# Squares of x moved from ScalarE and VectorE to GpSimd, a PSUM wait moved ahead of the pooling output, and two splits of the last stage issued earlier

## The reference

```python
def rms_norm(x, g):
    xf = x.astype(jnp.float32)
    y = xf * lax.rsqrt(jnp.mean(xf * xf, axis=-1, keepdims=True) + EPS)
    return (y * g.astype(jnp.float32)).astype(x.dtype)
...
    # first layer, with xn = rms_norm(h, pre_norm[0]) and h = x
    z = xn @ w_in
    u, g = jnp.split(z, 2, axis=-1)
    ...                     # pooled: window means of u, minus u, in four groups
    mixed = jnp.einsum('bsgc,gcd->bsgd', pooled, w_group).reshape(B, S, E_POOL)
    return (mixed * scale * jax.nn.silu(g)) @ w_out
...
    # last layer
    return (jax.nn.silu(g) * val) @ w_down
```

## Time and profile before

| | before |
|---|---|
| median of 3 runs | 2605.69 us |
| the profiled execution | 2608.29 us, with a span of 2606.3 us |
| PE busy | 2531.4 us (97%) |
| DVE busy | 1542.0 us (59%) |
| ACT busy | 1324.1 us (51%) |
| POOL busy | 99.4 us (4%) |
| DMA | 450.91 MB, mean 173 GB/s |
| granted TensorE clock, mean | 0.995 |

### The profile page before, as it was taken

The page is one execution under the profiler, slowest core; times in us unless marked ns, Lnnn a source line. Parts: engine busy times, 40 slices in busy tenths (PEclk is TensorE's granted clock), DMA queues, the critical chain, the costliest instruction groups (busy, mean ns, idle before and its releaser), DMA issues. The chain is left out here.

```text
span 2606.3 us, 35319 instructions
## 1 busy us (share of the span) xinstructions
PE 2531.4 (97%) x12930; PEld 2150.1 (82%) x12930; DVE 1542.0 (59%) x1817; ACT 1324.1 (51%) x1752; POOL 99.4 (4%) x156
## 2 busy tenths in 40 slices
PE   8999999999999999999899998899999999999998
PEld 7888888887779887778688887877888888888886
DVE  6665766644655555565555445655666666776554
ACT  5544444544556556464555445445554454554443
POOL 0000000000000001110000002000000000000010
PEclk9999999999999999999999999899999999999999
DMA  8666665555556660565566662054456666656563
GB/s 293 192 188 186 186 187 188 201 193 174 179 157 180 194 192 17 185 235 184 152 184 181 190 191 67 19 170 154 122 170 193 181 190 184 187 172 203 193 201 110
DMA packets 233421, 450.91 MB, mean 173 GB/s; under 512 B 14468, under 2 KB 59728, under 8 KB 232285
## 3 DMA queue, kind: packets, MB, share of 16 engines
q1 hardware_dynamic: 230518, 435.97, 53.9%
q0 software_dynamic: 2624, 13.27, 1.5%
q10 hardware_dynamic: 168, 0.19, 0.0%
HBM read 447.25 MB, written 2.12 MB: 172 GB/s over the span
## 5 line engine op out<-in xcount | busy, mean ns | idle before, releaser
L1445 DVE TENSOR_TENSOR w_lo<-raw,w_hi 128x1024 fp32r<-128x1024 f32 x852 | 1047.2, 1235 | 828.6 <-ACT w_hi L1007 809.7
L1007 ACT ACTIVATE w_hi<-raw 128x1024 fp32r<-128x1024 f32 x852 | 898.7, 1059 | 974.5 <-PE ps L620 616.0
L640 PE MATMUL ps<-x_hi_lo,w_hi 128*128 128x512 f32 x2336 | 823.7, 395 | 13.2 <-DVE w_lo L1445 13.2
L642 PE MATMUL ps<-x_hi_lo,w_lo 128*128 128x256 f32 x2336 | 661.7, 283 | 0.0
L640 PEld LDWEIGHTS ps<-x_hi_lo,w_hi 128*128 128x128 f32 x2336 | 440.0, 188 | 115.8 <-issue 9.0
L618 PE MATMUL ps<-w_hi,x_hi_lo 128*128 128x512 f32 (+3 forms) x1280 | 497.8, 389 | 21.3 <-DVE x_hi_lo L1474 12.4
L620 PE MATMUL ps<-w_hi,x_hi_lo 128*128 128x512 f32 (+3 forms) x1280 | 492.2, 385 | 0.0
L619 PE MATMUL ps<-w_lo,x_hi_lo 128*128 128x512 f32 (+3 forms) x1280 | 490.8, 383 | 0.0
L642 PEld LDWEIGHTS ps<-x_hi_lo,w_lo 128*128 128x128 f32 x2336 | 440.4, 189 | 0.0
L618 PEld LDWEIGHTS ps<-w_hi,x_hi_lo 128*128 128x128 f32 x1280 | 241.0, 188 | 76.7 <-issue 23.9
L620 PEld LDWEIGHTS ps<-w_hi,x_hi_lo 128*128 128x128 f32 x1280 | 240.8, 188 | 42.9
(11 more groups left out here) (306 smaller groups left out, 2237.8 us busy)
## 6 DMA issues: line engine op xcount, KB each, us to landing
raw<-in_w_up SPq DMA_DIRECT2D x160, 512.0 KB, 3.9
raw<-in_pool_w_in SPq DMA_DIRECT2D x128, 512.0 KB, 4.0
raw<-in_w_in SPq DMA_DIRECT2D x96, 480.0 KB, 4.0
raw<-in_w_down SPq DMA_DIRECT2D x76, 512.0 KB, 4.7
raw<-in_pool_w_out SPq DMA_DIRECT2D x64, 512.0 KB, 4.4
raw<-in_ple_w_gate SPq DMA_DIRECT2D x64, 512.0 KB, 3.9
raw<-in_mla_w_in SPq DMA_DIRECT2D x56, 448.0 KB, 4.0
raw<-in_pool_w_group SPq DMA_DIRECT2D x32, 512.0 KB, 4.3
```

Of the source, the lines that this page charges most:

```text
L640: pe.matmul(bank, w_hi[:, slot, cols], xs[:, k].rearrange("p s n -> p (s n)"), start=k == 0, stop=False, skip_group_check=True)
L642: last = pe.matmul(bank[:, 0:T], w_lo[:, slot, cols], xs[:, k, 0, :], start=False, stop=k == nkt - 1, skip_group_check=True)
L1007: act.activation(w_hi[:, u % RING, :], raw[:, slot, :], ACT.Copy).then_inc(S("w_hi"), 1)
L1445: dve.tensor_tensor(w_lo[:, u % RING, :], raw[:, u % RAW, :], w_hi[:, u % RING, :].bitcast(F32), ALU.subtract)\
```

## The change

The change has three parts.

1. *Squares.* ACT loses its eight square instructions and a first tiny copy. DVE loses the two adds. POOL gets seven instructions of 128x1024: a square of four tiles of x into `xsum`, then three times a square into `xsq` and an add onto `xsum`. They wait for the pieces of x and for one another. The loads of h are issued after them. The new tiles lie where `gate_in` and `mixed_group` come later.
2. *PSUM wait.* PE waits for the read-out of both last pooling chunks before the pooling output, no longer before the transposing of h.
3. *Last stage.* `hi(2)` ahead of `y_hi(4)` and `lo(2)` ahead of `y_lo(4)` go; the two units are handled after piece 5.

```diff
+    xsum = arena("x_square_sums", 78592, [128, 4, T])
+    xsq = arena("x_squares", 82688, [128, 4, T])
...
-                    last = pe.matmul(ps[:, 0, 0:T], onesq, xsq[:, n, :], start=n == 0, stop=n == 3)
+                    last = pe.matmul(ps[:, 0, 0:T], onesq, xsum[:, n, :], start=n == 0, stop=n == 3)
...
+        for c in (-2, -1):
+            n = CHUNKS_END["pool"] + c
+            pe.wait_ge(S(f"mm_free{n % 2}"), n // 2 + 2)
         pe.wait_ge(S("ident_in"), 16)
         ready_ple = split_ready("p_split")
         columns(yh, yl, 32, ready=lambda k: pe.wait_ge(S("y_lo"), Y_PIECES.index(k) + 1) if k in Y_PIECES else None)
...
-            if n == 0:
-                last = CHUNKS_END["pool"] - 1
-                pe.wait_ge(S(f"mm_free{last % 2}"), last // 2 + 2)
...
-        act.wait_ge(S("ones_square"), 1)
-        act.activation(junk[:, 0:1], onesq[:, 0:1], ACT.Copy)
         act.wait_ge(S("gains_in"), 16)
...
             split_hi(xh, xt, g, GAIN["pre0"])
             hi(1)
-            last = act.activation(xsq[:, 2 * g:2 * g + 2, :], xt[:, 2 * g:2 * g + 2, :], ACT.Square)
-        last.then_inc(S("x_squared"), 1)
...
-        hi(2)
         y_hi(4)
         hi(1)
         y_hi(5)
         for c in range(NCH):
-            skip(len(units_of(FKT)) - (0 if c else 3))
+            skip(len(units_of(FKT)) - (0 if c else 1))
...
-                lo(1)
-                dve.wait_ge(S("x_squared"), 1)
-                link(dve.tensor_tensor(xsq[:, 0:8, :], xsq[:, 0:8, :], xsq[:, 8:16, :], ALU.add))
-                lo(1)
-                dve.tensor_tensor(xsq[:, 0:4, :], xsq[:, 0:4, :], xsq[:, 4:8, :], ALU.add).then_inc(S("x_summed"), 1)
-                lo(3)
+                lo(5)
...
-        lo(2)
         y_lo(4)
         lo(1)
         y_lo(5)
         for c in range(NCH):
-            add_chunk(chunk(len(units_of(FKT)) - (0 if c else 3)), c * 512)
+            add_chunk(chunk(len(units_of(FKT)) - (0 if c else 1)), c * 512)
...
-        pool.wait_ge(S("x_squared"), 1)
+        for n, k in enumerate((0, 4, 8, 12)):
+            for piece in ((0, 1), (2,), (3,), (4,))[n]:
+                pool.wait_ge(S(f"x_in{piece}"), 16)
+            if n == 0:
+                pool.tensor_tensor(xsum, xt[:, 0:4, :], xt[:, 0:4, :], ALU.mult).then_inc(S("x_squares"), 1)
+            else:
+                pool.tensor_tensor(xsq, xt[:, k:k + 4, :], xt[:, k:k + 4, :], ALU.mult).then_inc(S("x_squares"), 1)
+                pool.wait_ge(S("x_squares"), 2 * n)
+                pool.tensor_tensor(xsum, xsum, xsq, ALU.add).then_inc(S("x_squares"), 1)
+                pool.wait_ge(S("x_squares"), 2 * n + 1)
+        pool.sem_inc(S("x_summed"), 1)
```

More of the change, by code:

```diff
@@ L228, in build @@
     xt = arena("x_features", 88064, [128, KT, T])
-    xsq = arena("x_squares", 32768, [128, KT, T])
+    xsum = arena("x_square_sums", 78592, [128, 4, T])
+    xsq = arena("x_squares", 82688, [128, 4, T])
     phl = arena("pooled_hi_lo", 88064, [128, 8, 2, T], F32R)
```

## The result

The changed kernel is slower: 2624.70 us against 2605.69 us (medians of five runs each), a difference of 19.0 us, with a ratio of 1.0072 (95% interval 1.0056 to 1.0088). One of the five runs of the changed kernel took 5063.95 us, and one of 21 of the kernel before beside the first experiments 5058.16 us, both at a full granted clock and for a reason that no trace here shows; the medians count them, the ratios leave them out. The profiled execution took 2627.47 us against 2608.29, 19.2 more, with a span of 2625.7 us.

What follows compares the result with a forecast made beforehand. PE, busy 97%, was taken as the bound: its stream plus its waits. Terms 0.1 + 11.5 + 1.9 + 2.8 + 2.6 + 1.4 = 20.3 us on the median 2605.69 gave 2626.0 us, range 2612 to 2633.

Steps and rivals of the forecast that it cites:

- Where the loss would be: PE waits at the start for the third and fourth unit, before the pooling output, and three units into the down product.
- (a): Rival, chance 0.14: POOL doesn't hold DVE up at the start; only 5.5 us lost, 2611.2 us.
- (d): Rival, chance 0.03: not slower, as ACT without its squares feeds PE earlier, so PE starts before 9.01 us.
- (e): Rival, chance 0.02: the waits before the pooling output and in the down product cost nothing; 2619.2 us.
- (b): Rival, chance 0.10: at the start POOL pauses between dependent instructions and DVE gets several turns; 8 to 15 us, about 2617.
- (c): Rival, chance 0.13: more loss, 23.7 us, by dearer POOL instructions, a longer slow spell at the start and both falls of the clock; 2629.4.
- both falls of the clock: Lower clock after both waits, before the pooling output and in the down product: 2.8 us, the upper end.
- the higher price: At the start, 2.54 us per POOL instruction instead of the forecast 2.3.
- Part 1, turns: At the start POOL and DVE instructions exclude each other, 2.3 us per POOL instruction; PE loses 11.5 us.
- The clock: Matmuls at the lower clock after PE's waits: 1.9 us at the start, 1.4 after one of the two later waits.
- Parts 2 and 3: PE waits 2.8 us before the pooling output and 2.6 us for the fourth unit of the down product.
- Gains of 0: At the start, squares off ACT, adds off DVE and later loads of h gain 0; PE waited for none of them.

Runs made afterwards that it cites:

- the first experiments: Follow-up runs of changed kernels, measured with 21 runs of the kernel before beside them on the same chip.
- reads against writes: Kernel before plus seven POOL adds of 128x1024 on tiles of no other use: 2615.57 us; plus 14 POOL memsets instead: 2606.90 us.
- two later starts: Kernel before with only the squares moved to POOL, begun after DVE's last split of x: 2617.24 us; begun after the rope angles: 2605.87 us.
- the run behind the rope angles: Kernel before with only the squares moved to POOL, begun after DVE's eleven tiny rope-angle instructions: 2605.87 us, 0.1 over before.
- the run with the squares later: Kernel before with only the squares moved to POOL, begun after DVE's last split of x: 2617.24 us, 11.2 over before.
- the run with half widths: Kernel before with only the squares moved to POOL, each POOL instruction cut into two of 128x512: 2612.49 us, 6.7 over before.

## Why the prediction was right

*Where the loss would be* held in all three places, and rivals (a), (d) and (e) fell: DVE was held up, PE began no earlier (9.18 against 9.01 us), and both later waits were real. Of (b), POOL didn't pause between its instructions; of (c), both falls of the clock came and the higher price didn't.

*Part 1, turns.* The mechanism is shown by reads against writes, and by two later starts. The size was too high: 11.5 us forecast, 8.2 measured up to the fourth unit. I priced every POOL instruction at 2.3 us from the earlier trace rows. From 12.65, where the second one began, to 27.01 POOL's six and DVE's four splits and one `w_lo` between them took 14.4 us; the forecast had 16.8 for them (13.4 to 30.2). Taking off DVE's share (4 x 0.44 + 1.15) leaves 1.9 us for a POOL instruction, an estimate. The spans that the profile gives to the adds, 2.4 us and more, are longer, and seem to hold some of DVE's turn. The other 0.75 us is the start: the second `w_lo` ended at 12.85, not at 13.4, and POOL began 0.2 us before that. So PE was idle 6.1 us there, not 9 to 10, and its first chunk ended near 44 us, not 47. Two small readings were off as well: PE asked for the third and fourth unit at 17.19 and 20.00, 0.1 us later than worked out, and its late start was gone by the second unit, which it began 0.7 us early.

*The clock.* Forecast 1.9 at the start and 1.4 for parts 2 and 3 together; measured in the profile 1.6, 2.8 and 1.6. I had let one of two waits of some 2.5 us end in a slow stretch, and both did, one of them of 6.8 us by the granted clock (6.1 of them with matmuls). The earlier trace rows hold 3.25 and 1.77 us and left that open; the waits between them go either way (last section). The two errors, -3.3 us for the turns and +2.7 us for the clock, nearly cancel: it is luck that 2626.0 came so close to 2624.7. The single terms were good to about 3 us, not to 1.3.

*Parts 2 and 3.* Waits of 2.8 and 2.6 us forecast, 3.0 and 2.6 measured.

*Gains of 0.* The moved squares, adds and loads of h gave nothing, as the run behind the rope angles shows: all of part 1 is in it, at 0.1 us (the interval reaches 2 us either way, but PE's waits up to 100 us are those of before).

## What to carry to other kernels

Work moved to GpSimd is not moved off VectorE where both read SBUF: count the VectorE instructions, not their microseconds, beside each GpSimd instruction, and put GpSimd where TensorE has several units in hand. A hand-written order holds leads that show in no busy time; ahead of a wait of ACT or DVE on each other, count how many units PE still has. A PE wait just behind the last matmul of a chunk cost the whole read-out here and, in both profiles where PE had nothing else to do, a stretch at the lower clock on top.

## What the runs showed of the hardware

A VectorE instruction of 128x2 or 128x64 with one tensor input (CAST, TENSOR_SCALAR) waits for a GpSimd instruction too: 1.89 to 2.30 us instead of 0.16 to 0.20. Beside memsets of GpSimd VectorE lost nothing. With such tiny instructions beside it, in the run with the squares later, GpSimd took 1.89 us for the square of a 128x1024 tile and 2.40 to 2.44 us for the sum of two tiles. Waits of PE of 2.4 to 2.9 us were followed by 3.4 to 6.8 us at the lower clock in these profiles, and so was, in the run with half widths, a third wait in a row of no more than 1.8 us. The length alone doesn't decide it: PE's wait for `qk_T` in the hybrid layer was 2.99 us before the change, with a granted clock of 0.66 from 1584 to 1589 us, and 2.96 after it, with 1.00 from 1598 to 1612.
